# Every third gathered expert row goes through ScalarE and GpSimd instead of TensorE

## The reference

```
u = expert_down[idx]                    # 128 rows of 1024 per token
act = gelu(sum_d h[d] * u[k, d])        # one dot product per expert
out[d] = sum_k gate[k] * act[k] * expert_up[idx[k], d]
```

## Time and profile before

| | |
|---|---|
| median of 3 runs | 4838.4 us (4838.11 to 4842.07) |
| the profiled execution | 4835.18 us, span 4833.4 us |
| PE, PEld busy | 3646.0 us (75%), 2152.9 us (45%) |
| DVE, ACT, POOL busy | 2797.6 us (58%), 1103.9 us (24%), 1151.9 us (24%) |
| mean granted TensorE clock | 0.886 of 2.4 GHz |
| gathered by GpSimd's queue | 1073.81 MB |

### The profile page before, as it was taken

One profiled execution on the slowest core, in us unless ns is written; L12 is line 12 of the kernel. 1 busy time (PEld: TensorE's weight loads), 2 busy tenths in 40 slices (PEclk: granted clock), 3 DMA queues, 4 the chain that ended last, 5 costly groups with the idle time before them and its releaser, 6 DMA issues. The chain is left out here.

```text
span 4833.4 us, 41734 instructions
## 1 busy us (share of the span) xinstructions
PE 3646.0 (75%) x13654; PEld 2152.9 (45%) x13654; DVE 2797.6 (58%) x6402; ACT 1103.9 (23%) x2607; POOL 1151.9 (24%) x1028
## 2 busy tenths in 40 slices
PE   4946699784767677788688686697868876677777
PEld 3834698463333232553366452452346653222222
DVE  5557755436844677555554457754555557755554
ACT  1104000121122122224432221232533221111111
POOL 0000000001423354222222123232222223343332
PEclk9978777887989999898899898798989999899999
DMA  4500000222978899787688687686669877899998
GB/s 176 185 27 3 4 1 5 68 69 111 408 310 345 348 414 408 296 314 270 246 315 316 246 310 308 233 325 224 244 237 338 303 294 308 341 373 420 414 420 361
DMA packets 202356, 1248.85 MB, mean 258 GB/s; under 512 B 24796, under 2 KB 29276, under 8 KB 67428
## 3 DMA queue, kind: packets, MB, share of 16 engines
q0 software_dynamic: 147456, 1073.81, 56.6%
q1 hardware_dynamic: 54184, 172.51, 10.7%
q10 hardware_dynamic: 512, 0.03, 0.0%
HBM read 1241.76 MB, written 4.46 MB: 258 GB/s over the span
## 5 line engine op out<-in xcount | busy, mean ns | idle before, releaser
L215 POOL DMA_INDIRECT held_pair<-in_experts,held_expert x1024 | 1151.7, 1125 | 3651.2 <-PE held_acc L233 2445.8
L277 DVE CUSTOM_DVE_ANT_0 held_pair<-held_pair,held_hrow 128x1024 f32<-128x1024 f32 x1024 | 1246.3, 1222 | 540.2 <-DMA held_pair<-in_experts,held_expert 494.0
L232 PE MATMUL held_acc<-held_pair,held_diag 128*128 128x512 f32 x2048 | 1146.3, 642 | 387.6 <-ACT held_diag L257 327.6
L233 PE MATMUL held_acc<-held_pair,held_diag 128*128 128x512 f32 x2048 | 1085.8, 613 | 0.0
L232 PEld LDWEIGHTS held_acc<-held_pair,held_diag 128*128 128x128 f32 x2048 | 351.3, 197 | 895.7 <-ACT held_diag L257 670.9
L257 ACT ACTIVATE held_diag<-held_ident,held_weight 128x128 f32<-128x128 f32 x1024 | 402.4, 394 | 1266.6 <-DVE held_weight L272 1233.9
L233 PEld LDWEIGHTS held_acc<-held_pair,held_diag 128*128 128x128 f32 x2048 | 404.2, 197 | 520.8 <-issue 520.8
L250 ACT ACTIVATE held_bent<-held_dot 128x2 f32<-128x2 f32 x512 | 102.8, 201 | 540.7 <-DVE held_dot L277 502.1
L500 PE MATMUL pgh_ps<-pgh_hhi,pgh_whi 128*128 128x256 f32 x384 | 127.4, 332 | 28.9 <-DVE pgh_wlo L519 28.9
L500 PE MATMUL p2h_ps<-p2h_hhi,p2h_whi 128*128 128x256 f32 x368 | 123.4, 335 | 31.0 <-DVE p2h_wlo L519 31.0
L1284 PE MATMUL c_ps<-c_keys,held_room 128*128 128x128 f32 x256 | 45.3, 359 | 131.0 <-DMA c_iota<-in_iota 131.0
(11 more groups left out here) (516 smaller groups left out, 5509.1 us busy)
## 6 DMA issues: line engine op xcount, KB each, us to landing
pgh_raw<-in_w_in SPq DMA_DIRECT2D x48, 512.0 KB, 6.7
p2h_raw<-in_w_in SPq DMA_DIRECT2D x46, 512.0 KB
p_raw<-in_w_in SPq DMA_DIRECT2D x34, 512.0 KB, 3.5
p_w_ada<-in_w_ada SPq DMA_DIRECT2D x16, 1024.0 KB, 6.3
held_pair<-in_experts,held_expert POOLq DMA_INDIRECT x1024
e2qh_raw<-in_w_peer_q SPq DMA_DIRECT2D x32, 512.0 KB, 8.0
ada_w<-in_w_ada SPq DMA_DIRECT2D x4, 2048.0 KB, 11.3
e1q_raw<-in_w_query SPq DMA_DIRECT2D x16, 512.0 KB, 3.7
```

The lines of the kernel that those rows point to most:

```text
L215: pool.indirect_dma_start(self.pair[m % BUFS][:], None, self.layers[t // TT][0], bass.IndirectOffsetOnAxis(ap=self.expert[:, t % TT, s:s + ...
L232: pe.matmul(self.acc[0][:], diag[:], up[:, 0:512], start=s == 0, stop=s == NJ - 1)
L233: pe.matmul(self.acc[1][:], diag[:], up[:, 512:D], start=s == 0, stop=s == NJ - 1).then_inc(self.added, 1)
L277: ins = dve.tensor_tensor_reduce(down, down, self.hrow[:, t % TT, :], 1.0, 0.0, ALU.mult, ALU.add, self.dot[:, t % 2, s:s + 1])
```

## The change

A slot m with m % 3 == 2 (341 of 1024) no longer goes to TensorE. ScalarE scales its up row in place by the slot's weight, and GpSimd adds the row to a new buffer `side` (a copy for the first such slot of a tile), ahead of the transfer of the same beat. At the end of a tile two matmuls by the identity add `side` into the PSUM banks. The other slots are as before, with four diagonals in place of six. To make room for `side`, `mv` of the memory stages and `fq` of the forgetting attention move into parts of held tiles that are free then. `MIXER_LENGTHS` is set anew. Worked out from the lengths, the beats per stage (they are the same in both halves):

| stage | n3 | p2 | hn | vt | forget | foxa | swaa | mema | pg | mg | po | n4 | q | c4, c6 | c5 | c7 |
|---|---|---|---|---|---|---|---|---|---|---|---|---|---|---|---|---|
| before | 4 | 33 | 14 | 2 | 8 | 27 | 17 | 7 | 34 | 19 | 12 | 4 | 23 | 38 | 14 | 48 |
| after | 6 | 32 | 15 | 4 | 9 | 26 | 19 | 10 | 32 | 20 | 12 | 7 | 22 | 28 | 14 | 48 |

c1 58, mn 8, mp 48, mh 11, mt 4, c23 137 and the drain 222 stay.

```diff
@@ -173,14 +173,25 @@
                 dve.tensor_tensor(mod[:, 0:4 * groups], ps[:, 0:4 * groups], bcol[:, 0:4 * groups], ALU.add)
 
 
-GROUP, BUFS, DIAGS = 2, 8, 6
+GROUP, BUFS, DIAGS = 2, 8, 4
 TILES, SLOTS = 2 * TT, 2 * TT * NJ
 BENT_AT = GROUP
 WEIGH_AT = GROUP + 1
 DIAG_AT = WEIGH_AT
 UP_AT = DIAG_AT + 1
 AHEAD = BUFS - UP_AT
-BEATS = SLOTS + UP_AT + 6
+TAIL = UP_AT + 6
+BEATS = SLOTS + TAIL
+
+
+def on_pool(m):
+
+    return m % 3 == 2
+
+
+def pe_slots(m):
+
+    return m - m // 3
 
 
 class Gather:
@@ -189,14 +200,14 @@
 
     def __init__(self, r, k, xT, layers):
         self.k, self.xT, self.layers = k, xT, layers
-        self.hrow, self.sums = r.sb("hrow", [P, TT, D]), r.sb("sums", [P, D])
+        self.hrow, self.sums, self.side = r.sb("hrow", [P, TT, D]), r.sb("sums", [P, D]), r.sb("side", [P, D])
         self.pair = [r.sb(f"pair{u}", [P, 2 * D]) for u in range(BUFS)]
         self.diag = [r.sb(f"diag{u}", [P, P]) for u in range(DIAGS)]
         self.expert, self.gate = r.sb("expert", [P, TT, NJ], U32), r.sb("gate", [P, TT, NJ])
         self.dot, self.bent, self.weight = r.sb("dot", [P, 2, NJ]), r.sb("bent", [P, 2, NJ]), r.sb("weight", [P, 2, NJ])
         self.acc, self.pt = [r.ps(f"acc{u}") for u in range(2)], r.ps("turn")
-        self.chosen, self.dotted, self.bent_made, self.weighed, self.diag_made, self.added, self.kept, self.turned, self.moved = r.sem(
-            "chosen", "dotted", "bent_made", "weighed", "diag_made", "added", "kept", "turned", "moved")
+        self.chosen, self.dotted, self.bent_made, self.weighed, self.diag_made, self.added, self.kept, self.turned, self.moved, self.scaled, self.sided, self.joined = r.sem(
+            "chosen", "dotted", "bent_made", "weighed", "diag_made", "added", "kept", "turned", "moved", "scaled", "sided", "joined")
         self.landed = [r.sem(f"landed{u}") for u in range(BUFS)]
 
     def tile_end(self, n, later):
@@ -205,13 +216,30 @@
         return t if s == NJ - 1 and 0 <= t < TILES else None
 
     def pool(self, pool, n):
+        m = n - UP_AT
+        if 0 <= m < SLOTS and on_pool(m):
+            t, s = divmod(m, NJ)
+            up = self.pair[m % BUFS][:, D:2 * D]
+            done = m // 3
+            pool.wait_ge(self.scaled, done + 1)
+            if done:
+                pool.wait_ge(self.sided, done)
+            if s < 3:
+                if t:
+                    pool.wait_ge(self.joined, t)
+                pool.tensor_copy(self.side[:], up).then_inc(self.sided, 1)
+            else:
+                pool.tensor_tensor(self.side[:], up, self.side[:], ALU.add).then_inc(self.sided, 1)
         for m in range(0 if n == 0 else n + AHEAD, n + AHEAD + 1):
             if m < SLOTS:
                 t, s = divmod(m, NJ)
                 if s == 0:
                     pool.wait_ge(self.chosen, t + 1)
                 if m >= BUFS:
-                    pool.wait_ge(self.added, m - BUFS + 1)
+                    if on_pool(m - BUFS):
+                        pool.wait_ge(self.sided, (m - BUFS) // 3 + 1)
+                    else:
+                        pool.wait_ge(self.added, pe_slots(m - BUFS + 1))
                 pool.indirect_dma_start(self.pair[m % BUFS][:], None, self.layers[t // TT][0],
                                         bass.IndirectOffsetOnAxis(ap=self.expert[:, t % TT, s:s + 1], axis=0)).then_inc(self.landed[m % BUFS], 16)
 
@@ -225,12 +253,20 @@
         m = n - UP_AT
         if 0 <= m < SLOTS:
             t, s = divmod(m, NJ)
-            pe.wait_ge(self.diag_made, m + 1)
-            if s == 0 and t:
+            first = pe_slots(m) == pe_slots(t * NJ)
+            if first and t and not on_pool(m):
                 pe.wait_ge(self.kept, 2 * t)
-            up, diag = self.pair[m % BUFS][:, D:2 * D], self.diag[m % DIAGS]
-            pe.matmul(self.acc[0][:], diag[:], up[:, 0:512], start=s == 0, stop=s == NJ - 1)
-            pe.matmul(self.acc[1][:], diag[:], up[:, 512:D], start=s == 0, stop=s == NJ - 1).then_inc(self.added, 1)
+            if not on_pool(m):
+                j = pe_slots(m)
+                pe.wait_ge(self.diag_made, j + 1)
+                up, diag = self.pair[m % BUFS][:, D:2 * D], self.diag[j % DIAGS]
+                pe.matmul(self.acc[0][:], diag[:], up[:, 0:512], start=first, stop=False)
+                pe.matmul(self.acc[1][:], diag[:], up[:, 512:D], start=first, stop=False).then_inc(self.added, 1)
+        t = self.tile_end(n, 0)
+        if t is not None:
+            pe.wait_ge(self.sided, (t + 1) * NJ // 3)
+            pe.matmul(self.acc[0][:], self.k.ident[:], self.side[:, 0:512], start=False, stop=True)
+            pe.matmul(self.acc[1][:], self.k.ident[:], self.side[:, 512:D], start=False, stop=True).then_inc(self.joined, 1)
         for u in range(2):
             t = self.tile_end(n, 2 + 2 * u)
             if t is not None:
@@ -249,15 +285,21 @@
             act.wait_ge(self.dotted, g + 1)
             act.activation(self.bent[:, t % 2, at], self.dot[:, t % 2, at], self.layers[t // TT][1]).then_inc(self.bent_made, 1)
         m = n - DIAG_AT
-        if 0 <= m < SLOTS:
+        if 0 <= m < SLOTS and not on_pool(m):
             t, s = divmod(m, NJ)
+            j = pe_slots(m)
             act.wait_ge(self.weighed, m // GROUP + 1)
-            if m >= DIAGS:
-                act.wait_ge(self.added, m - DIAGS + 1)
-            act.activation(self.diag[m % DIAGS][:], self.k.ident[:], ACT.Copy, scale=self.weight[:, t % 2, s:s + 1]).then_inc(self.diag_made, 1)
+            if j >= DIAGS:
+                act.wait_ge(self.added, j - DIAGS + 1)
+            act.activation(self.diag[j % DIAGS][:], self.k.ident[:], ACT.Copy, scale=self.weight[:, t % 2, s:s + 1]).then_inc(self.diag_made, 1)
+        if 0 <= m < SLOTS and on_pool(m):
+            t, s = divmod(m, NJ)
+            up = self.pair[m % BUFS][:, D:2 * D]
+            act.wait_ge(self.weighed, m // GROUP + 1)
+            act.activation(up, up, ACT.Copy, scale=self.weight[:, t % 2, s:s + 1]).then_inc(self.scaled, 1)
         t = self.tile_end(n, 1)
         if t is not None:
-            act.wait_ge(self.added, (t + 1) * NJ)
+            act.wait_ge(self.joined, t + 1)
             if t:
                 act.wait_ge(self.turned, 2 * t)
             for u in range(2):
@@ -1583,17 +1625,15 @@
...
-        mkv, mv = hT[:, :, NMEM:2 * NMEM], a.sb("mv", [P, 4, 2, P])
...
+    mkv, mv = hT[:, :, NMEM:2 * NMEM], hT[:, 0:4, 0:NMEM].rearrange("p h (j n) -> p h j n", n=P)
...
@@ -1632,9 +1672,9 @@
                    + [(tiles_of(z[:, Y_SKV + 1, :]), v[:, 4, first:first + HTILES])], beats=beats["vt"])
         with ExitStack() as fox:
             a = Room(nc, fox, own("fox"))
-            fq, fk = a.sb("fq", [66, FH // 2, HALF]), a.sb("fk", [66, FH // 2, now.stop])
+            fq, fk = room[0:66, 3 * DC + 4:3 * DC + 8, :], a.sb("fk", [66, FH // 2, now.stop])
             lanes = lambda head: slice(head % 2 * 64, head % 2 * 64 + 2)
-            forget_stage(nc, own("forget"), k, z, cols("b_forget")[0:FH], fq[:], fk[:], past.low, past.last_sum, now, beats["forget"])
+            forget_stage(nc, own("forget"), k, z, cols("b_forget")[0:FH], fq, fk[:], past.low, past.last_sum, now, beats["forget"])
             items = []
             for c in range(FH // 2):
                 for t, head in [(t, 2 * c + o) for t in tiles for o in range(2)]:
@@ -1670,8 +1710,8 @@
     norm_stage(nc, own("n4"), k, x, DC, D, cols("norm2_g_2"), h, tokens=HALF, beats=beats["n4"])
 
 
-MIXER_LENGTHS = {"n3": 5, "p2": 35, "hn": 15, "vt": 2, "forget": 9, "foxa": 28, "swaa": 18, "mema": 8, "pg": 36, "mg": 20, "po": 13, "n4": 5,
-                 "q": 24, "choose": 40}
+MIXER_LENGTHS = {"n3": 8, "p2": 36, "hn": 18, "vt": 4, "forget": 10, "foxa": 30, "swaa": 22, "mema": 12, "pg": 36, "mg": 23, "po": 14, "n4": 8,
+                 "q": 25, "choose": 32}
 
 
 def experts_and_second_mixer(nc, r, k, ins, cols, xT, hT, mod):
@@ -1679,8 +1719,8 @@
     layers = [(ins["experts1"], ACT.Gelu_apprx_tanh, mod[:, 5 * DC:6 * DC]), (ins["experts2"], ACT.Gelu, None)]
     room = r.sb("room", [P, 2 * PH * S // HALF, HALF])
     memory = nc.dram_tensor("memory_scratch", [P, 8, NMEM], F32, kind="Internal").ap()
-    half_done = HTILES * NJ + UP_AT + 6
-    first_layer_done = TT * NJ + UP_AT + 6
+    half_done = HTILES * NJ + TAIL
+    first_layer_done = TT * NJ + TAIL
     keys_of_first = lambda c: c % 2
     keys_of_second = lambda c: c
     at = lambda t: (t, t % TT * P)
```

More of the change, by code:

```diff
@@ L1584, in memory_stages @@
 def memory_stages(nc, k, ins, cols, hT, kept_in_dram, beats):
-    with ExitStack() as memory:
-        a = Room(nc, memory, "mem")
-        mT = hT[:, :, 0:NMEM]
-        mkv, mv = hT[:, :, NMEM:2 * NMEM], a.sb("mv", [P, 4, 2, P])
-        load_stage(nc, "meml", [(mT, ins["memT"].rearrange("(c p) t -> p c t", p=P))])
-        norm_stage(nc, "mn", k, mT, DC, D, cols("mem_norm_g_2"), mT, tokens=NMEM, beats=beats["mn"])
```

(14 more changed lines are left out.)

## The result

The changed kernel takes 5063.4 us (median of 4 runs, 5053.7 to 5068.5) against 4840.2 us for the kernel before on the same chip: ratio 1.0448, 95% interval 1.0432 to 1.0464. It is 4.5% slower, where 3.5% faster was forecast, and the time lies outside the range. The profiled run took 5068.1 us.

A forecast was written before the change was run, and what follows sets the result against it. Transfers were taken to bound c1, c23 and the drain, TensorE p2, pg, mg, po and q, neither the rest. Halves of -91.5 and -89.5, +6 and +5 gave -170 us: 4668 us, 3.5% less; range 4595 to 4770.

The forecast's parts named there:

- VectorE, "nothing is added": VectorE's program gets no new work; its dots might wait for GpSimd's adds: +8 us in c23, hidden in the drain.
- The rival of the shared port: GpSimd's adds and VectorE's two-input work exclude each other: some +99 us, giving 4767 us; chance 0.14.
- The add at 2.29 us: GpSimd's time for one add, taken from VectorE's time for twice the elements; it leaves room in drain and c23.
- The rival in which GpSimd becomes the pace: Adds over 4.6 us in the drain or 4.3 in c1 and c23 hold back transfers: 4898 us; chance 0.08.
- TensorE's relief: 341 slots leave TensorE, 583 us of its work; time is saved only in stages where TensorE paces.
- p2, pg, q: the step: TensorE's saving, limited by the transfers' rate: p2 -16, pg -20, q -13.5 us per half.
- the last sentence of the prediction: Signs of being wrong, among them TensorE idle in p2 released by w_lo, meaning late weight loads; no size given.
- "half of TensorE's saving": Attention group: of 41 us saved by TensorE, half counted because of loads, barriers and eight more beats: -20 us per half.
- The forecast's own terms for them, +18 and -34: Price of moved beats over both halves: n3 and n4 gain beats, +18 us; c4 and c6 lose ten each, -34.
- Tile ends: ScalarE and TensorE wait some 3 us where a tile's last slot is GpSimd's, three tiles in eight: +5 us.
- the drain does stay at 550 us: The drain, transfer-bound, changes by 0 us, even if TensorE's granted clock fell to the 1.2 GHz level.
- ScalarE's scaling: Scaling an up row costs 1057 ns against 394 for a diagonal, 227 us more in all, taken as hidden.

The follow-up runs named there:

- e1: The changed kernel with GpSimd's adds into side left out, ScalarE's scaling and all waits kept: 4786.6 us, ratio 0.9891.
- e2: The changed kernel with two GpSimd memsets, which only write, in place of each add: 4831.3 us, ratio 0.9981.
- e7: The changed kernel with two GpSimd copies that read the scaled up row in place of each add: 4975.8 us, ratio 1.0271.
- e6: The changed kernel with VectorE scaling and adding the up row in one instruction, without ScalarE's scaling or GpSimd's add: 4932.3 us, ratio 1.0181.
- e5: e1 with a third raw-weight buffer for p2, pg, po and q, and side left out: 4725.3 us, ratio 0.9755.
- e4: The kernel before with only the new table of stage lengths (beats): 4848.1 us, ratio 1.0014.
- run c1: The kernel before, old lengths, with 107 slots' up rows scaled and added by VectorE in seven stages, plus a third raw-weight buffer: 4724.7 us, ratio 0.9743.

## Why the prediction was wrong

It had two errors of different size, and e1 parts them: the adds' side effects (277 us) and the gain, which was 54 instead of 170 us.

**VectorE, "nothing is added".** This is the step that failed and turned the sign: the prediction charged VectorE's delay with under 20 us in all, and the adds cost 277 us, some 230 of them by keeping VectorE out. The lock was seen and priced at +8 us in c23 and as hidden in the drain, since VectorE's busy time of 441 us would still be under 550. The busy time did stay under it, 392 of 595 us, and the drain grew by 45. The reasoning took a share of busy time for slack. A slot's buffer comes back only after its dot, gelu, weights, scaling and add in turn, and the add came to hold up the dots of the slots behind it as well. What is shown is that the same waits with 1.93 us of writing cost nothing in the drain (e2, 550.7 us), that with reading they do (e7, 560.5; after, 595.4), and that VectorE's own work without any lock costs time there too, at 61% busy (e6, 584.0). That it is the ring of eight buffers that carries this is argued from the order of the waits; no run had more buffers. The rival of the shared port had the right mechanism and 99 us instead of some 230: it multiplied by the chance of meeting VectorE at work and left out the drain's 74 adds and everything queued behind a held dot. Past the queue time of e2 it is 232 / 341 = 0.68 us a slot against the rival's 0.37.

**GpSimd.** The add at 2.29 us was sound (2.45 on average, 2.34 for the shortest); the estimate of 2.25 from the figure of the Trainium skill (GPSIMD Engine Reference, 3.1 Elementwise — side-by-side cycle accounting) was nearly as good. The rival in which GpSimd becomes the pace fell: it needed an add of over 4.6 us, and e2, with 1.93 us of GpSimd's time a slot, loses 45 us, hardly any in the drain.

**TensorE's relief.** Of the sum, with the adds out (e1 minus before, both halves; forecast in brackets): p2 -13 (-32), pg -21 (-40), q -16 (-27), mg and po -28 (-30), the attention group +39 (-40), n3 and n4 +23 (+18), c4 and c6 -37 (-34), the other stages -10 (+10, and +5 for tile ends). That sums to -62.5 us, by profiled executions; by medians it is -54.
- p2, pg, q: the step named the next limit as the transfers' rate and left out the latency of the weight loads over two buffers, which the last sentence of the prediction holds only as a sign to look for. e5 shows it: with a third buffer these three reach 246, 253 and 179 us, -34, -40 and -25, the forecast's own figures.
- The attention group: "half of TensorE's saving" was wrong by 79 us. With TensorE's work kept, the eight beats a half more cost 38 us (e4); taking a third of its slots off TensorE gave nothing back (711 us in e1 as in e4; 676 in run c1 against 672 before). In foxa the granted clock fell with the load; for the rest of the group the cause is open.
- The beats moved for no net gain, as e4 shows, 8 us slower and the interval just above no change. The forecast's own terms for them, +18 and -34, were good, and the attention group's beats were what it had not priced.
- Tile ends: their last slot is a GpSimd one in two tiles of eight (slots 383 and 767), not three, so the +5 us was a little high; no run measures it.

**The rest.** Without the adds the drain does stay at 550 us with TensorE at a granted clock of 0.85 (e1), as forecast. ScalarE's scaling took 1141 ns where 1057 was assumed; no run leaves it out alone, so that it delayed nothing is not shown. Nor does a run move the buffers alone; with them moved, the memory stages mn to mt take 235 us in e1 against 241 before.

## What to carry to other kernels

Moving work to GpSimd is not moving it off VectorE: before pricing it, count VectorE's SBUF-to-SBUF work in the same stretch, and test with memsets (writes) against copies (reads), which parts queue time from the port. An engine's idle share in a ring of buffers is not slack if its work is a link in the buffer's return: here each us added to VectorE's time, by the lock or by work of its own, cost 0.37 to 0.49 us. And when the bound of a loop is relieved, ask what latency its other buffers were sized to hide: the third weight buffer was worth 0 us before the relief and 43 to 61 after it.
